# Late modulation weights of the first mixer: products and sums on VectorE, the sum over partitions on TensorE

## The reference

```python
mod_lat = split(silu(c) @ w_mod + b_mod, 6)           # first block: 1024 -> 6144
...
mod = silu(c_2) @ w_ada + b_ada                        # second block: 1024 -> 6144
shf, scf = split(silu(c_2) @ w_ada_f + b_ada_f, 2)     # end: 1024 -> 2048
...
lat = split_cols(h_lat @ w_in); ctx = split_cols(h_ctx @ w_in)   # q, kv, hgrn q, z, v, gates
```

## Time and profile before

| what | us |
|---|---|
| runs | 2390.17, 2393.74, 2392.65; median 2392.65 |
| profiled execution, its own time | 2396.66 |
| its span, first to last instruction | 2395.4 |
| TensorE busy (matmuls) | 2130.4 |
| VectorE busy | 595.4 |
| mean granted TensorE clock | 0.945 of full speed |
| projections from hq to the end of v, with ten modulation pieces | 100.94 to 313.11 |
| state stage | 313.11 to 342.08 |
| levels | 355.06 to 439.46 |

### The profile page before, as it was taken

The page is one execution under the profiler, slowest core; times in us unless marked ns, Lnnn a source line. Parts: engine busy times, 40 slices in busy tenths (PEclk is TensorE's granted clock), DMA queues, the critical chain, the costliest instruction groups (busy, mean ns, idle before and its releaser), DMA issues.

```text
span 2395.4 us, 22902 instructions
## 1 busy us (share of the span) xinstructions
PE 2130.4 (89%) x9781; PEld 1111.8 (46%) x9781; DVE 595.4 (25%) x1168; ACT 322.7 (13%) x697; POOL 134.6 (6%) x193
## 2 busy tenths in 40 slices
PE   3999979989978999999989999988789797779996
PEld 1654447665444333333333333333567696453332
DVE  2010308424132111111111111110363553331112
ACT  1010121112101111111101111110122111011111
POOL 3010113200000000000000000000200100000100
PEclk7999989999988999999999999999899897879998
DMA  7453359141338999999999999997431200259994
GB/s 285 166 200 141 141 211 358 35 146 36 106 133 355 390 427 428 428 426 428 428 428 427 428 428 427 427 428 332 161 119 71 106 1 1 105 235 422 420 421 179
DMA packets 90971, 648.61 MB, mean 271 GB/s; under 512 B 9568, under 2 KB 14872, under 8 KB 47056
## 3 DMA queue, kind: packets, MB, share of 16 engines
q1 hardware_dynamic: 86320, 640.40, 65.3%
q0 software_dynamic: 4544, 6.66, 0.9%
HBM read 645.92 MB, written 1.11 MB: 270 GB/s over the span
## 4 chain that ended last, share of the span: by engine, by line
PE 77%; DMA 13%; DVE 5%; ACT 3%; issue 2%; POOL 0%; SPq 0%; POOLq 0%; ACTq 0%; DVEq 0%
PE ps L211 37%; PE ps L1466 13%; DMA sb<-in_w_gate_up 7%; PE ps L1493 6%; PE ps L2273 5%; DMA sb<-in_w_down 5%; PE ps L1223 4%; PE ps L2297 2%; PE ps L535 2%; PE ps L423 2%; PE ps L216 2%; PE ps L1455 2%; PE ps L584 0%; DMA sb<-in_w_in 0%; DMA sb<-in_w_mod 0%
## 5 line engine op out<-in xcount | busy, mean ns | idle before, releaser
L211 PE MATMUL ps<-sb 128*128 128x128 f32 (+7 forms) x3942 | 904.0, 395 | 104.5 <-DVE sb L2218 13.7
L211 PEld LDWEIGHTS ps<-sb 128*128 128x128 f32 (+1 forms) x3942 | 631.9, 202 | 366.1 <-issue 248.7
L1466 PE MATMUL ps<-sb 128*64 128x512 f32 x2048 | 453.0, 598 | 4.2 <-DMA sb<-in_w_gate_up 3.3
L1466 PEld LDWEIGHTS ps<-sb 128*64 128x64 f32 x2048 | 143.9, 138 | 311.9 <-issue 291.1
L1493 PE MATMUL ps<-sb 128*64 128x512 f32 x1024 | 231.7, 607 | 51.0 <-DMA sb<-in_w_down 28.0
L1593 DVE TENSOR_SCALAR sb<-ps 128x512 f32<-128x512 f32 x32 | 33.6, 1049 | 798.1 <-PE ps L1466 798.1
L1493 PEld LDWEIGHTS ps<-sb 128*64 128x64 f32 x1024 | 86.8, 140 | 185.0 <-issue 185.0
L216 PE MATMUL ps<-sb 128*128 128x128 f32 x455 | 80.9, 319 | 69.2 <-DVE sb L873 17.5
L216 PEld LDWEIGHTS ps<-sb 128*128 128x128 f32 x455 | 60.0, 166 | 131.6 <-issue 68.5
L2273 PE MATMUL ps<-sb 128*64 128x512 f32 x512 | 115.2, 603 | 5.4 <-POOL sb L2382 4.0
L1223 PE MATMUL ps<-sb 128*128 128x512 f32 x256 | 115.4, 593 | 1.6 <-ACT sb L2365 1.0
(11 more groups left out here) (325 smaller groups left out, 1042.4 us busy)
## 6 DMA issues: line engine op xcount, KB each, us to landing
sb<-in_w_gate_up SPq DMA_DIRECT2D x128, 2048.0 KB, 24.9
sb<-in_w_down SPq DMA_DIRECT2D x64, 2048.0 KB, 26.5
sb<-in_w_in SPq DMA_DIRECT2D x24, 2048.0 KB, 8.4
sb<-in_w1e SPq DMA_DIRECT2D x32, 1024.0 KB, 16.0
sb<-in_w3e SPq DMA_DIRECT2D x32, 1024.0 KB, 18.2
sb<-in_w2e SPq DMA_DIRECT2D x32, 1024.0 KB, 20.8
sb<-in_w_mod SPq DMA_DIRECT2D x12, 2048.0 KB, 7.6
sb<-in_w_ada SPq DMA_DIRECT2D x12, 2048.0 KB, 8.5
```

Source lines behind the costliest of these rows:

```text
L211: last = te.matmul(o, l, r, start=i == 0, stop=i == len(pairs) - 1)
L1466: last = te.matmul(ps[64 * h:64 * h + 64, 512 * c:512 * c + 512], xg[k][:, t, 64 * m:64 * m + 64], w[:, at:at + 512], start=False, stop=t ...
```

## The change

Each late block r is now handled in eight halves of a former piece: half m has r = m // 8 and row group t = m % 8, 2048 columns, 1 MB. VectorE multiplies half t by its column of `ccol` (one number in each partition) and adds it to a sum `msum[r % 2]` of 128 × 2048 (`add_half`). The first of a block is a `tensor_scalar`, the other seven are `scalar_tensor_tensor`. TensorE then multiplies the finished sum by a column of ones: four matmuls for each block, once.

The ring of the projections keeps two slots. The halves get a ring `rm` of four: the two halves of the third slot, `kgt`, and `gss[1]`. SP's list is rewritten, and so are the places of `add_half` in VectorE's list and of `modulate(r)` in TensorE's: r = 0 between the two halves of hq, r = 1 to 4 in the middle of the four pieces of z, r = 5 in the middle of v0. VectorE waits for block 5 before its scans, because they write where `msum[1]` and a slot of the ring lie. All `step()` calls are gone.

```diff
+        def add_half(m):
+            r, t = m // 8, m % 8
+            a = msum[r % 2]
+            c = ccol[:, 0 if r < 2 else 2, t:t + 1]
+            ve.wait_ge(w_full[rm.slot(m)], rm.turn(m))
+            if t:
+                ve.wait_ge(s["msum"], m)
+                ve.scalar_tensor_tensor(a, rm.view(m), c, a, MUL, ADD).then_inc(s["msum"], 1)
+            else:
+                if r > 1:
+                    ve.wait_ge(*full_at(("mod", r - 2)))
+                ve.tensor_scalar(a, rm.view(m), c, None, MUL).then_inc(s["msum"], 1)
...
+        rm = SlotTable([None, None, slots[2][:, 0:2048], slots[2][:, 2048:4096], kgt.rearrange("p a b -> p (a b)"),
+                        gss[1].rearrange("p h t -> p (h t)")], r1.after(), ids=(2, 3, 4, 5))
+        for m in range(48):
...
+            rm.add(flat, mod_src[r + 1].rearrange("a (p t) n -> (a p) t n", t=8)[:, t, at:at + 2048], (s["msum"], m + 1))
...
-            for n in range(4, len(r1.loads)):
+            load(0, r1)
+            load(1, r1)
+            for m in range(3):
+                load(m, rm)
+            sp.wait_ge(s["mask"], 1)
+            load(3, rm)
+            m = 4
+            for n in range(2, len(r1.loads)):
+                upto = (6, 8, 10, 12, 16, 20, 28, 36, 44, 48)[n - 2] if n < 12 else 48
+                while m < upto:
+                    load(m, rm)
+                    m += 1
                 load(n, r1)
...
+        def modulate(r):
+            te.wait_ge(s["msum"], 8 * r + 8)
+            o = opened(("mod", r))
+            for j in range(4):
+                last = te.matmul(o[32 * j:32 * j + 1, :], ones[:, 0:1], msum[r % 2][:, 512 * j:512 * j + 512],
+                                 start=True, stop=True, tile_position=(0, 32 * j))
+            last.then_inc(is_full(("mod", r)), 1)
...
-            step()
-            for c in range(2):
-                by_feature(256, [("hq", 4 * c + f) for f in range(4)], weights(next(order), r1))
-                step()
+            by_feature(256, [("hq", f) for f in range(4)], weights(next(order), r1))
+            modulate(0)
+            by_feature(256, [("hq", 4 + f) for f in range(4)], weights(next(order), r1))
             for d in range(2):
                 for c in range(2):
-                    by_feature(512, [("z", d, 4 * c + f) for f in range(4)], weights(next(order), r1))
-                    step()
-            for c in range(2):
-                by_token(512, [("v", c, i) for i in range(4)], weights(next(order), r1))
-                step()
+                    w = weights(next(order), r1)
+                    by_feature(512, [("z", d, 4 * c + f) for f in range(2)], w)
+                    modulate(1 + 2 * d + c)
+                    by_feature(512, [("z", d, 4 * c + f) for f in (2, 3)], w)
+            w = weights(next(order), r1)
+            by_token(512, [("v", 0, i) for i in range(2)], w)
+            modulate(5)
+            by_token(512, [("v", 0, i) for i in (2, 3)], w)
+            by_token(512, [("v", 1, i) for i in range(4)], weights(next(order), r1))
...
+            for m in range(2):
+                add_half(m)
             o = filled(ve, "krp")
...
             t_lb = dv.n
+            for m in range(2, 8):
+                add_half(m)
             for f in range(8):
+                add_half(8 + f)
                 ve.wait_ge(s["qt"], f + 1)
...
             for d in range(2):
                 for f in range(8):
+                    for m in range(2):
+                        add_half(16 + 16 * d + 2 * f + m)
                     ve.wait_ge(*read_at(("z", d, f)))
...
             ve.wait_ge(s["zf"], 16)
+            ve.wait_ge(*full_at(("mod", 5)))
             for d in range(2):
                 hgrn_scan(d)
```

More of the change, by code:

```diff
@@ L100, with __init__ @@
 class SlotTable:
-    def __init__(self, slots, base, parts=1):
-        self.slots, self.base, self.parts, self.loads = slots, base, parts, []
+    def __init__(self, slots, base, parts=1, ids=range(7)):
+        self.slots, self.base, self.parts, self.loads = [slots[i] for i in ids], base, parts, []
+        self.ids = list(ids)
     def add(self, view, src, freed):
@@ L109, in slot @@
     def slot(self, n):
-        return n % len(self.slots)
+        return self.ids[n % len(self.slots)]
     def turn(self, n):
@@ L115, in view @@
     def view(self, n):
-        return self.loads[n][0](self.slots[self.slot(n)])
+        return self.loads[n][0](self.slots[n % len(self.slots)])
     def after(self):
         n, k = len(self.loads), len(self.slots)
-        return [b + self.parts * ((n - i + k - 1) // k) for i, b in zip(range(k), self.base)] + list(self.base[k:])
+        total = list(self.base)
+        for at, i in enumerate(self.ids):
+            total[i] += self.parts * ((n - at + k - 1) // k)
+        return total
 SEMS = """c x ctx con cm b_mod gains rows0 rows more wr b_late0 b_late1 mod_out0 mod_out1 mod_first mcol1 ctanh cc sq rstd
-    xn dve pool mask mod_w mrow lb0 lb1 qt zf qh kg KG st_half hg_ks hg_up kr hgn z_qr osum gt qn qrn scmx mg ymd x1
+    xn dve pool mask mod_w msum mrow lb0 lb1 qt zf qh kg KG st_half hg_ks hg_up kr hgn z_qr osum gt qn qrn scmx mg ymd x1
     row2 mcol
@@ L305, in build @@
         slots = [sb[:, COLS - 4096 * (i + 1):COLS - 4096 * i] for i in range(NS)]
-        r1 = SlotTable(slots[0:3], [0] * NS)
+        r0 = SlotTable(slots, [0] * NS, ids=range(3))
         w_in = rows8(I["w_in"])
         mod_src = [I["w_mod"]] * 3 + [I["w_ada_2"]] * 3 + [I["w_ada_f_2"].unsqueeze(0)]
[L310 to L314, removed]
+        for q in range(4):
+            w = mod_src[0].rearrange("a (p t) n -> (a p) t n", t=8)
+            r0.add(two, w[:, 2 * q:2 * q + 2, 0:2048], (s["mod_w"], q + 1) if q < 3 else full_at(("mod", -1)))
+        r1 = SlotTable(slots, r0.after(), ids=(1, 0))
         def add_cols(w, at, width, last_use):
             r1.add(eight(width), w[:, :, at:at + width], full_at(last_use))
-        for q in range(4):
-            add_mod(-1, q)
         add_cols(w_in, 768, 320, "kr")
@@ L397, in sync_mix1 @@
             for n in range(4):
-                load(n, r1)
+                load(n, r0)
             sp.wait_ge(*read_at(("mod", -1)))
@@ L462, in tensor_mix1 @@
             for q in range(4):
-                modulate(next(order), -1, q)
+                modulate_first(q)
             for t in (6, 7):
@@ L785, in pool_mix1 @@
             late_bias(0)
+            gp.wait_ge(s["kr"], 1)
             late_bias(1)
@@ L1424, in build @@
         bank.lay([2, 3], moe1)
-        r2 = SlotTable(slots, r1.after())
+        r2 = SlotTable(slots, rm.after())
         def add_gate_up(e):
@@ L1704, in build @@
         bank.lay([0, 1, 2, 3, 6, 7], mix2)
-        r3 = SlotTable(slots[0:2], r2.after())
+        r3 = SlotTable(slots, r2.after(), ids=range(2))
         w_in2 = I["w_in_2"].rearrange("a (p t) n -> (a p) t n", t=8)
@@ L2247, in build @@
         bank.lay([2, 3], moe2)
-        r4 = SlotTable(slots, r3.after(), 2)
+        r4 = SlotTable(slots, r3.after(), parts=2)
         for p in range(17):
```

53 lines of the change are left out of this document (20 added, 33 removed).

## The result

The changed kernel takes 2440.7 us (median of four runs, 2438.84 to 2443.08), against 2392.49 for the kernel before, run beside it: ratio 1.0203, 95% interval [1.0185, 1.0221]. It is slower by 48 us, where the forecast was slower by 12. The profiled execution took 2438.84 us, 42.2 more than the profiled one of before.

A forecast was written before the change was run, and what follows sets the result against it. TensorE, busy 89% of the span, was taken to bound the kernel wherever a stage waits for it. Projections +42.9, state stage −10.2 and levels −20.6 gave +12.1 us, a median of 2404.7; range 2389 to 2420.

The forecast's parts named there:

- the first hq half: Projections: its load stands behind halves 6 and 7, so TensorE stands for 16.0 us.
- the four middle stops: In z01, z10, z11 and v0, TensorE waits 6.6 us each for a block's halves and last sum, 26.4 us.
- The sum of VectorE: Adding one half over 2048 float32 columns takes 2.29 us, as the product of two tensors; lower bound 1.23.
- the clock behind the stops: Projections: each of the five stops costs 2.65 us more at the lower clock, 13.2 us in all.
- state stage: Between projections and levels: four groups without the pieces take 18.8 us in place of 29.0, 10.2 less.
- the way to the levels: From the state stage to the levels, 342.08 to 355.06 before: it stays.
- cold state stage: Rival, chance 0.10: the clock falls in the state stage, 13 us more, at 2418.
- serial loads: Rival, chance 0.04: each load pays 1.9 us for itself, not once for the queue; 34 us more, at 2439.
- the clock in the levels: TensorE's share is 3.7 of 4 us, clock expected to hold; levels take 63.8 us, 20.6 less.
- The 39.9 us: Levels: VectorE's six products summed over all 14 half levels, the twelve middle ones taken between 3.60 and 2.56 us.
- the 38 us of saved TensorE work: Whole kernel: 24 pieces, 43.9 us, go and closing products, 5.5, come in; 38 us faster if nothing else happened.

The follow-up runs named there:

- k5_level0: k2_order plus four unused 512-column matmuls behind each of the two half levels of l = 0 only; 2356.27 us, ratio 0.9834.
- k10_halfgap: As k9_onegap, with one unused 64-column matmul in place of four; 2388.26 us, ratio 0.998.
- k2_order: The changed kernel with only SP's load order altered: first hq load ahead of halves 6 and 7, later halves issued one load sooner; 2387.78 us, ratio 0.9976.
- k8_burst: k2_order plus one burst of sixteen unused 512-column matmuls behind the second half level of l = 3; 2373.83 us, ratio 0.9911.
- k9_onegap: Load order of k7_half, with four unused 64-column matmuls once, behind the second half level of l = 0; 2382.68 us, ratio 0.9952.
- k4_thin: The kernel before, with the eleven modulation pieces in the levels writing 16 columns in place of 512; 2406.34 us, ratio 1.0065.
- k7_half: k2_order with z00's load ahead of halves 10 and 11, and four unused 256-column matmuls behind each half level but the last two; 2356.3 us, ratio 0.9845.
- k6_narrow: k2_order plus four unused 64-column matmuls behind each half level but the last two; 2357.74 us, ratio 0.9845.

## Why the prediction was wrong

**Right: the first hq half.** A stop of 16.0 us was forecast, 15.91 came, by the steps named: two sums of 2.36 that free the buffers, SP, then the queue.

**Right in place, 0.9 us short in size: the four middle stops.** Forecast 6.6 each, measured 7.50 to 7.57. The queue needs nearly the forecast 18.1 us: from the issue of z10's load at 175.81 to the landing of the last half at 194.15 it is 18.3. The rest is on VectorE: its short steps hold the sums up, and the last begins at 194.61, 0.5 behind its landing. The sum of VectorE was right too: 2.349 us against the 2.29 taken from the product of two tensors.

**A little too dear: the clock behind the stops.** The projections took 255.6, less 194.0 for the work, 5.8 for the products and 46.0 for the five stops: 9.8 us, 2.0 a stop and not 2.65 (the first hq half took 16.19 where 14.01 is the full clock). This and the size of the stops cancel: 255.6 against 255.1.

**Right: state stage, the way to the levels, all behind them.** 31.6 against 18.8 + 13.0 = 31.8. The cold state stage did not come. That rival had more for it than the prediction says: it looked at the window at 322 alone, and in the kernel before the clock is at 0.50 from 332 to 336, behind a stop of 2.48 us in this very stage. Nor did the serial loads: five loads behind each other still make a stop of 7.5 and not of 14, and the four halves issued from 176.41 to 178.15 land 2.3 to 2.7 us apart. The Trainium skill gives a DMA on the software path a fixed part of about 2.0 us in "DMA: Bandwidth & Descriptors", section "Anatomy of one DMA — SWDGE (gpsimd) path". These loads run in a hardware queue (SP's), and here a part of that size, 1.9 us, shows once for the queue and not once for each load.

**Wrong: the clock in the levels.** The failed step is "TensorE's share there is 3.7 of 4 us, so I expect the clock to hold". The time at the full clock was right (63.8 forecast, 63.65 in k5_level0 with its 1.9 us of fillers beside VectorE), but the levels took 95.5, all but the first two half levels at 0.50: 31.7 us more. Without these, 2440.7 would be 2409.0, 4.3 us from the forecast. Two things were overlooked, and both stood in the trace of before. First, the prediction's own terms give a stop ahead of the second level: VectorE needs 3.7 + 0.6 + 3.6 = 7.9 us from the first matmul, TensorE's two half levels 7.4. I used these numbers for the length of a half level and did not read the difference, 0.5 us, as a stop; it came at 0.83 us. That gaps of 0.6 us keep the clock was read from the 128-column products of the state stage; in the levels a stop of 0.61 us went ahead of the fall (k10_halfgap). Second, the half level of 7.02 us behind a gap was priced like the 5.3 us behind the gap ahead of 348.65, as a cost that is over after a while of work. The windows of the kernel before, behind that gap (columns as in the earlier trace rows), tell more:

```profile
428.00:432.00 4.00, 4.00 (x20) 4.00 (x21) 2.02 (x6) 0.00 (x0) 0.00 (x0) 0.50 0.02 4
432.00:436.00 4.00, 4.00 (x20) 3.90 (x19) 3.26 (x7) 0.58 (x1) 0.00 (x0) 0.50 0.00 0
436.00:440.00 4.00, 2.61 (x21) 2.40 (x21) 2.59 (x4) 1.76 (x3) 0.00 (x0) 1.00 0.00 0
```

TensorE worked from 425.65 on without a break, and the clock came back only behind the 128-column products that begin at 432.46. It was the one place before where the levels' matmuls ran cold, at 0.50, and in their 7 us they did not come out of it. It is also where no modulation piece stood any more: the last one ends at 415.84, and the stop comes one pair of half levels later. A loss was priced per stop that in this stretch lasts to its end.

One reading of the levels was wrong without harm. Of the twelve half levels between the first and the last, three do not lie between 3.60 and 2.56 us: VectorE's six products take 5.81 (from 375.88), 5.41 (from 398.06) and 5.30 (from 420.22), each time while GpSimd adds a bias (373.99, 396.16 and 418.33, 6 us each). The 39.9 us hold only with these three at the length of their neighbours. The 63.8 came out all the same, since GpSimd adds nothing during the levels of the changed kernel. The third of the three is also what made the stop of 2.53 us ahead of 425.65.

The Trainium skill has the neighbouring rule, in "TensorE: Matmul & The Clock Gate", section "A second HAM failure mode: psum-queue depth-cycling": in a bf16 kernel of 512-column matmuls TensorE idled briefly between groups of matmuls, and its clock fell and came back again and again. The trace agrees on the fall, behind stops of 0.61 to 1.04 us, but not on what follows: no swinging, 80.8 us at 0.50.

**The range.** It reached to 2420 by a cold state stage and closed the levels off. A rival "cold levels" (14 half levels at 7.0 us, 98) would have stood at some 2439, beside the 2440.7 measured; I gave that time only to the serial loads (2439), a mechanism that is not there; that this rival's number lies near the measured one is chance.

**What stays open.** Why the clock falls behind 0.61 us in one run and not behind 0.84 in another, and what in a stream of 64-column matmuls keeps it from regaining the clock that it can hold. The runs show both and explain neither. One rival is untested: that it counts how soon a stop comes behind the stretch at 0.50 ahead of the levels. By the windows of 2 to 5 us, the stops of 0.83 (after, k2_order, k8_burst) and 0.61 us (k10_halfgap) begin 8 to 9 us after the clock came back there, and it fell; of those some 13 us after, it fell behind 1.04 (k9_onegap) and held over 0.84 (k4_thin); at 18 us it held over 0.51 (k5_level0). No run changes this alone.

**A version that beats both kernels.** k5_level0 and k7_half take 2356.3 us: 1.5 to 1.7% less than the kernel before, and 84 us less than the change as made. That is 39 us less than the kernel before measured beside them. It is near the 38 us of saved TensorE work in the prediction, but in part by chance: in the levels VectorE sets the pace, and not what TensorE has to do.

## What to carry over

When work is taken off TensorE, look at what it filled: a piece that only seems to cost TensorE's time may be what keeps it from waiting for VectorE, and the clock may hang on that. Price a lost clock by the stretch behind the stop, not by the stop: ask which matmuls come next, and look in the trace for a place where this very stream ran at 0.50 and when it came out of it. And when loads are cut finer and go in one queue with others, write down for each the wait that stands ahead of it; here one row of ten numbers was worth 53 us.

## What the runs showed of the hardware that I had not expected

- A stream of 64-column float32 matmuls on 128x128 weights held 2.4 GHz for 62 us (k6_narrow), but at 1.2 GHz it did not come out of that in 80.8 us of unbroken work (after). 4.58 us of 512-column matmuls brought the clock back (k8_burst).
- The clock fell behind stops as short as 0.83, 1.04 and 0.61 us (after, k9_onegap, k10_halfgap), and not behind 0.52 (k5_level0) or 0.84 (k4_thin) in the same stream, nor behind 2.21 ahead of 512-column matmuls (k2_order) or 1.73 ahead of 128-column ones (k5_level0).
- Useless work can shorten a kernel: 1.9 us of it saved 31.5 (k5_level0 against k2_order).
- VectorE's products of 128x512 float32, 0.68 us each, took up to 1.75 us while GpSimd added a bias (before, at 377 and 421). Only the coincidence is shown.
